# Roots and reciprocals for the norms of a two-block model, gates at eviction and an earlier weight load

## What is computed

```python
def rmsnorm(x, g):
    y = xf * lax.rsqrt(jnp.mean(xf * xf, axis=-1, keepdims=True) + EPS)
# first stack, per layer
    h = rmsnorm(x, g_pre_mix); y = token_mixer(h, ...)      # mLSTM heads and attention, ends in w_out
    x = x + rmsnorm(y, g_post_mix)
    h = rmsnorm(x, g_pre_ffn); y = conv_ffn(h, ...)
    x = x + rmsnorm(y, g_post_ffn)
# second stack, per layer
    ax = modulate(rmsnorm_2(h, norm1_g), mx[0], mx[1])      # then w_in, pooling, attention, retention
    yn = (y - mu) * lax.rsqrt(var + EPS) * gn_g             # retention_output, per head of 64
    ret = silu(gate) * yn                                   # then w_out
    h = h + mx[5] * conv_ffn_2(modulate(rmsnorm_2(h, norm2_g), mx[3], mx[4]), ...)
return rmsnorm_2(h, final_g)
```

## Time and profile before

| | |
|---|---|
| median of three runs | 2932.6 (2928.62 to 2936.35) |
| the profiled execution's own time | 2934.65 |
| its span, first to last instruction | 2932.9 |
| mean granted clock of PE | 0.995 |
| DMA | 269.95 MB, mean 92 GB/s |
| table loads of ACT at L382 | 13, of 1283 ns each |

### The profile page before, as it was taken

One profiled execution on the slowest core, in us unless ns is written; L12 is line 12 of the kernel. 1 busy time (PEld: TensorE's weight loads), 2 busy tenths in 40 slices (PEclk: granted clock), 3 DMA queues, 4 the chain that ended last, 5 costly groups with the idle time before them and its releaser, 6 DMA issues. The chain is left out here.

```text
span 2932.9 us, 35827 instructions
## 1 busy us (share of the span) xinstructions
PE 2856.3 (97%) x14618; PEld 2408.2 (82%) x14618; DVE 1763.2 (60%) x2639; ACT 1160.9 (40%) x1709; POOL 150.0 (5%) x172
## 2 busy tenths in 40 slices
PE   9999999999999999999988999999999999999999
PEld 7657888878467888889965999999999975788887
DVE  6667866768567767667665565435534137564563
ACT  5255524443345424342255343213323236543342
POOL 0101000010110000000020100000000002100001
PEclk9999999999999999999999999999999999999999
DMA  5303243343112243326620111121122220232322
GB/s 204 108 15 108 93 134 105 93 130 122 44 59 86 90 147 100 116 85 232 212 66 30 58 58 65 57 73 65 58 58 65 65 97 23 101 101 84 111 83 83
DMA packets 84180, 269.95 MB, mean 92 GB/s; under 512 B 9264, under 2 KB 12208, under 8 KB 83632
## 3 DMA queue, kind: packets, MB, share of 16 engines
q1 hardware_dynamic: 84016, 267.66, 27.9%
HBM read 265.52 MB, written 2.10 MB: 91 GB/s over the span
## 5 line engine op out<-in xcount | busy, mean ns | idle before, releaser
L1011 PE MATMUL PS<-HH,WH 128*128 128x512 f32 (+1 forms) x3032 | 997.9, 366 | 23.7 <-DVE WL L856 8.1
L1011 PE MATMUL PS<-HH,WL 128*128 128x512 f32 (+1 forms) x3032 | 992.9, 364 | 0.0
L1011 PE MATMUL PS<-HL,WH 128*128 128x512 f32 (+1 forms) x3032 | 992.5, 364 | 0.0
L856 DVE TENSOR_TENSOR WL<-STAGE,WH 128x1024 fp32r<-128x1024 f32 (+2 forms) x420 | 482.7, 1151 | 497.5 <-ACT WH L850 497.2
L850 ACT ACTIVATE WH<-STAGE 128x1024 fp32r<-128x1024 f32 (+2 forms) x420 | 407.3, 973 | 621.5 <-DMA STAGE<-in_w_down 274.0
L1011 PEld LDWEIGHTS PS<-HH,WH 128*128 128x128 f32 x3032 | 559.5, 188 | 95.1 <-issue 11.9
L1011 PEld LDWEIGHTS PS<-HL,WH 128*128 128x128 f32 x3032 | 559.9, 188 | 65.4 <-issue 1.9
L1011 PEld LDWEIGHTS PS<-HH,WL 128*128 128x128 f32 x3032 | 559.7, 188 | 64.7
L1011 PE MATMUL PS<-GH,WL 128*128 128x512 f32 (+1 forms) x880 | 294.7, 367 | 0.0
L1011 PE MATMUL PS<-GL,WH 128*128 128x512 f32 (+1 forms) x880 | 294.7, 367 | 0.0
L1011 PE MATMUL PS<-GH,WH 128*128 128x512 f32 (+1 forms) x880 | 294.6, 367 | 0.0
(11 more groups left out here) (233 smaller groups left out, 2544.9 us busy)
## 6 DMA issues: line engine op xcount, KB each, us to landing
STAGE<-in_w_up SPq DMA_DIRECT2D x176, 512.0 KB, 3.3
MODBUF<-in_w_mod SPq DMA_DIRECT2D x96, 512.0 KB, 4.2
STAGE<-in_w_in SPq DMA_DIRECT2D x84, 512.0 KB, 3.4
STAGE<-in_w_down SPq DMA_DIRECT2D x64, 384.0 KB, 3.1
STAGE<-in_w_down SPq DMA_DIRECT2D x64, 320.0 KB, 2.9
STAGE<-in_w_out SPq DMA_DIRECT2D x32, 512.0 KB, 4.7
BM<-in_na_bias SPq DMA_DIRECT2D x24, 256.0 KB, 2.6
CR<-in_const_ret SPq DMA_DIRECT2D x2, 1152.0 KB, 5.2
```

The lines of the kernel that those rows point to most:

```text
L856: dve.tensor_tensor(WL[unit.slot][:, 0:size], STAGE[unit.slot][:, 0:size], WH[unit.slot][:, 0:size].bitcast(F32), ALU.subtract).then_inc(w ...
L1011: ins = pe.matmul(self.acc(tile, col, tn), w[:, c:c + P], r[:, k, t0:t0 + tn], start=(k == 0 and m == 0), stop=(k == seg.kc - 1 and m == 2))
```

## The change

- In `Rstd`, ACT takes a square root and DVE a reciprocal of RSTD in place; the same in `MixHead` and `RetentionHead`. The table set asked for is `sqrt_and_others` instead of `natural_log`, at fewer places. What waited for the logarithm waits for the root.
- `in2` evicts the three gate tiles through Silu (`store_gates`) instead of Copy, and the Silu of `RetentionHead` goes. The exp set is asked for at the end of `in2`.
- `attention_and_retention` gets the next `Run` and loads its first four units in its tail; unit 0 is also split there. PTN0 and PWM move to slot 2's start.
- Orders: the pooling products go before the last but one retention product; the mean of a late norm goes before chunk 2 of its tile instead of chunk 4; the third tile runs three chunks behind for 768 tokens too; the modulation products of in2(0) are 2 for the first two tiles and 4 for the others.

```diff
 class Rstd:
-                act.activation(RSTD[:, 0:n], PS[2][:, 0:n], ACT.Ln, bias=EPSC[:, 0:1]).then_inc(log_done.sem, 1)
-                act.wait_ge(log_done.sem, log_done.at(self.n + 1))
-                act.activation(RSTD[:, 0:n], RSTD[:, 0:n], ACT.Exp, scale=-0.5).then_inc(rstd_done.sem, 1)
+                act.activation(RSTD[:, 0:n], PS[2][:, 0:n], ACT.Sqrt, bias=EPSC[:, 0:1]).then_inc(root_done.sem, 1)
             def wait(self, eng):
+                eng.wait_ge(root_done.sem, root_done.at(self.n + 1))
+                eng.reciprocal(RSTD[:, 0:self.tokens], RSTD[:, 0:self.tokens]).then_inc(rstd_done.sem, 1)
                 eng.wait_ge(rstd_done.sem, rstd_done.at(self.n + 1))
 class MixHead, act and dve:
-                act.activation(MEAN2, MEAN2, ACT.Ln, scale=float(D // P)).then_inc(head_ln.sem, 1)
+                act.activation(MEAN2, MEAN2, ACT.Sqrt, scale=float(D // P)).then_inc(head_root.sem, 1)
                 self.copied(act, 3)
-                act.wait_ge(head_ln.sem, head_ln.at(1))
-                act.activation(MEAN2, MEAN2, ACT.Exp, scale=-0.5).then_inc(head_rstd.sem, 1)
...
+                dve.wait_ge(head_root.sem, head_root.at(1))
+                dve.reciprocal(MEAN2, MEAN2).then_inc(head_rstd.sem, 1)
                 self.low(dve, 3)
 class RetentionHead, act:
-                act.activation(Z[:, RG:RG + 3, 0:n], Z[:, RG:RG + 3, 0:n], ACT.Silu).then_inc(gate_done.sem, 1)
-                act.preload_act_table_set("natural_log")
                 self.copied(act, 0)
                 self.copied(act, 1)
-                self.run.split_high(act, 0)
...
-                    act.activation(GROUP[c][:, 0:n], PS[VAR_PS[c]][:, 0:n], ACT.Ln,
-                                   bias=EPSC[:, 0:1]).then_inc(group_ln.sem, 1)
+                    act.activation(GROUP[c][:, 0:n], PS[VAR_PS[c]][:, 0:n], ACT.Sqrt,
+                                   bias=EPSC[:, 0:1]).then_inc(group_root.sem, 1)
                 self.run.split_high(act, 2)
-                for c in range(3):
-                    act.wait_ge(group_ln.sem, group_ln.at(c + 1))
-                    act.activation(GROUP[c][:, 0:n], GROUP[c][:, 0:n], ACT.Exp, scale=-0.5).then_inc(group_rstd.sem, 1)
 class RetentionHead, dve:
-                self.low(dve, 0)
-                self.run.split_low(dve, 0)
-                for c in range(1, 5):
+                for c in range(5):
                     self.low(dve, c)
                 self.run.split_low(dve, 1)
-                self.run.split_low(dve, 2)
-                dve.wait_ge(gate_done.sem, gate_done.at(1))
                 for c in range(3):
+                    dve.wait_ge(group_root.sem, group_root.at(c + 1))
+                    dve.reciprocal(GROUP[c][:, 0:n], GROUP[c][:, 0:n]).then_inc(group_rstd.sem, 1)
...
+                    if c == 0:
+                        self.run.split_low(dve, 2)
 Run.tensor:
-                        behind = 3 if self.opening else 0
+                        behind = 0 if i or head.begins else 3 if self.opening or seg.tokens == TOK else 0
...
-                                if t == 0 and k == 4 and i == 0 and head.late:
+                                if t == 0 and k == 2 and i == 0 and head.late:
 PoolPrep.act:
+                if tile.ends:
+                    act.preload_act_table_set("exp_and_others")
 attention_and_retention, sync, then scalar and vector:
                     sp.wait_ge(rest_in.sem, rest_in.at(32))
+                    ahead.loaded = 4
+                    sp.wait_ge(pv_done.sem, pv_done.at(U))
+                    ahead.load(sp, 0)
+                    ahead.load(sp, 1)
+                    sp.wait_ge(masked.sem, masked.at(4 * PAIRS))
+                    ahead.load(sp, 3)
+                    sp.wait_ge(y_ps.sem, y_ps.at(1))
+                    ahead.load(sp, 2)
...
+                        if s == U - 1:
+                            act.preload_act_table_set("sqrt_and_others")
                         if s == U + 1:
                             pooled()
+                            ahead.split_high(act, 0)
...
+                    ahead.split_low(dve, 0)
 store_gates, new, in in2's second segment:
+            def put(act, t, acc):
+                if t < RG - N2_KV:
+                    return other(act, t, acc)
+                return act.activation(by_bank(Z[:, t + N2_KV, 0:tokens], tokens), acc, ACT.Silu)
 in2:
-                            mods=None if l else lambda t: 4 if t < 8 else 3),
+                            mods=None if l else lambda t: 2 if t < 2 else 4),
```

More of the change, by code:

```diff
@@ L246, in build @@
         ysq_done, ysq_added = S("ysq_done"), S("ysq_added")
-        log_done, rstd_done = S("log_done"), S("rstd_done")
+        root_done, rstd_done = S("root_done"), S("rstd_done")
         xsq_done, xsq_summed = S("xsq_done"), S("xsq_summed")
@@ L379, in act, with wait_root @@
                 n = self.tokens
-                act.activation(RSTD[:, 0:n], PS[2][:, 0:n], ACT.Ln, bias=EPSC[:, 0:1]).then_inc(log_done.sem, 1)
-                act.wait_ge(log_done.sem, log_done.at(self.n + 1))
-                act.activation(RSTD[:, 0:n], RSTD[:, 0:n], ACT.Exp, scale=-0.5).then_inc(rstd_done.sem, 1)
-            def wait_log(self, eng):
-                eng.wait_ge(log_done.sem, log_done.at(self.n + 1))
+                act.activation(RSTD[:, 0:n], PS[2][:, 0:n], ACT.Sqrt, bias=EPSC[:, 0:1]).then_inc(root_done.sem, 1)
+            def wait_root(self, eng):
+                eng.wait_ge(root_done.sem, root_done.at(self.n + 1))
             def wait(self, eng):
+                eng.wait_ge(root_done.sem, root_done.at(self.n + 1))
+                eng.reciprocal(RSTD[:, 0:self.tokens], RSTD[:, 0:self.tokens]).then_inc(rstd_done.sem, 1)
                 eng.wait_ge(rstd_done.sem, rstd_done.at(self.n + 1))
@@ L581, in begin @@
                             ins.then_inc(var_ps.sem, 1)
-                        pe.wait_ge(group_ln.sem, group_ln.at(3))
+                        pe.wait_ge(group_root.sem, group_root.at(3))
                     for k in range(5):
@@ L592, in build @@
         ROWS2 = [PO, PO + 1, NV, NV + 1, NV + 2, RG, RG + 1, RG + 2]
-        mean_ps, centred, group_sq, var_ps, group_ln, group_rstd, group_out, gate_done = (
-            S(n) for n in ("mean_ps", "centred", "group_sq", "var_ps", "group_ln", "group_rstd", "group_out", "gate_done"))
+        mean_ps, centred, group_sq, var_ps, group_root, group_rstd, group_out = (
+            S(n) for n in ("mean_ps", "centred", "group_sq", "var_ps", "group_root", "group_rstd", "group_out"))
         def scale_y(dve, gain, c):
@@ L744, in pe @@
                 if self.gain:
-                    self.first.wait_log(pe)
+                    self.first.wait_root(pe)
                     for c in range(DC):
@@ L1149, in stream @@
             if parts[0][0].ready:
-                done(head_ln=1, head_rstd=1, head_ps=4, hg_done=4, head_out=4)
+                done(head_root=1, head_rstd=1, head_ps=4, hg_done=4, head_out=4)
             elif parts[0][0].begins:
-                done(mean_ps=3, centred=3, group_sq=3, var_ps=3, group_ln=3, group_rstd=3, group_out=6, gate_done=1)
+                done(mean_ps=3, centred=3, group_sq=3, var_ps=3, group_root=3, group_rstd=3, group_out=6)
             done(**{f"w_loaded{s}": 16 * len(range(s, n, ring)) for s in range(ring)}, w_hi=n, w_lo=n, unit_done=n,
@@ L1156, in stream @@
                  sq_done=run.n_sq, sq_added=run.n_added, sq_summed=run.n_summed,
-                 ysq_done=run.n_ysq, ysq_added=run.n_ysum, log_done=run.n_rstd,
+                 ysq_done=run.n_ysq, ysq_added=run.n_ysum, root_done=run.n_rstd,
                  rstd_done=run.n_rstd, xsq_done=run.n_x, xsq_summed=run.n_x, t_done=run.n_t, h_hi=run.n_h,
@@ L1192, in build @@
         qk_own, conv_done, qk_done = S("qk_own"), S("conv_done"), S("qk_done")
-        head_ln, head_rstd, head_ps, hg_done, head_out = (
-            S(n) for n in ("head_ln", "head_rstd", "head_ps", "hg_done", "head_out"))
+        head_root, head_rstd, head_ps, hg_done, head_out = (
+            S(n) for n in ("head_root", "head_rstd", "head_ps", "hg_done", "head_out"))
         ROWS1 = [AQ1, AQ1 + 1, AQ1 + 2, AQ1 + 3, V1, V1 + 1, V1 + 2, V1 + 3]
@@ L1212, in pe @@
                 if tile.t == 7:
-                    tile.seg.head.late.wait_log(pe)
+                    tile.seg.head.late.wait_root(pe)
                     pe.wait_ge(acc_free.sem, acc_free.at(tile.n - 6))
@@ L1665, in build @@
         VTN = st("VTN", [P, 9, 3 * P])
-        PTN0 = st("PTN0", [P, 2, SEQ])
-        PWM = st("PWM", [P, 2, P])
+        PTN0 = sb("PTN0", [P, 2, SEQ], offset=o_slot[2])
+        PWM = sb("PWM", [P, 2, P], offset=o_slot[2] + 2 * SEQ * 4)
         BM = [sb(f"BM{i}", [P, 2 * PAIR], offset=o_slot[3] + i * 2 * PAIR * 4) for i in range(4)]
@@ L1773, in build, with attention_and_retention @@
         KE = CS[:, C_KE:C_KE + 4]
-        def attention_and_retention(tokens, VEC, layer):
```

(27 more changed lines are left out.)

4 lines of the change are left out of this document (1 added, 3 removed).

## The result

The changed kernel takes **2985.7 us** (median of 4 runs, 2982.8 to 2986.8) against 2933.4 of the kernel before beside it: ratio 1.0179, 95% interval 1.0163 to 1.0195. That is 52.3 us slower, where +42 was forecast. The profiled execution took 2986.0 with a span of 2984.3, so 51.4 of span over the one before; its mean granted clock is 0.985, before 0.995.

What follows compares the result with a forecast made beforehand. TensorE, busy 97%, was taken as the bound, with what is left at the seams. 20.1 + 7.2 + 9.5 + 4.6 + 2.4 - 1.6 = +42 on 2934.7 gave 2977, against the median 2975 us; range 2914 to 2999.

Steps and rivals of the forecast that it cites:

- Rate of the reciprocal: VectorE's reciprocal in place of Exp: 6.3 ns an element, 3.38 us for 128x512 and 4.99 us for 128x768.
- Nine seams: Nine places where a root mean square stands between TensorE and its next matmul: together +20.1 us.
- rival 1: Reciprocal runs at the rate of other VectorE operations, 0.69 and 0.96 us: -16, 2917 us; chance 0.19.
- rival 2: Reciprocal makes eight passes for an element, 4.4 and 6.5 us: +62, 2995 us; chance 0.18.
- rival 3: Cheap middle, reciprocal at 4.2 ns an element, 2.3 and 3.4 us: 2951 us; chance 0.57 together with the forecast.
- rival 4: The change doesn't do what it says: tables still reload between Sqrt and Square or Identity; chance 0.02.
- Clock: Half clock after longer pauses at the six seams a stream follows, part of it in the pause: 1.2 each, +7.2 us.
- RetentionHead, layer 0: Three reciprocals in turn on VectorE before low(5), on which chunk 5 waits: +8.3 us and 1.2 of clock.
- PE then starts at about 1597.6: RetentionHead, layer 0: TensorE starts at 1597.6 instead of 1598.58, its variance products at 1602.75 instead of 1604.40.
- Layer 1: RetentionHead in layer 1, the same three reciprocals in turn: +3.4 us and 1.2 of clock.
- Gates at eviction: End of in2: load back to exp after the last eviction, ahead of the block's barrier: 1.2 twice, +2.4 us.
- Orders: Pauses of 1.33 and 1.60 us go; against it at most 1.5 at three heads: -1.6 us with 0.2 of rounding.

Runs made afterwards that it cites:

- run 4: Whole model left out, only VectorE reciprocals and adds of 2 to 768 elements: reciprocal 6.25 ns an element from 128 up.
- Run 1: The kernel before with the square roots and reciprocals alone: 2993.98 us, ratio 1.0204.
- run 5: The changed kernel with more idle TensorE matmuls ahead of the seams (42, 37 or 30 calls for 24): 2968.68 us, ratio 1.0122 to the kernel before.
- run 9: The kernel of run 8 with the load back to the exp set moved to the attention block's front: 2911.31 us, ratio 0.9926 to the kernel before.
- run 10: The kernel before with one table set for Ln and Exp and the change's three orders: 2916.22 us, ratio 0.9936.
- run 8: The changed kernel with all inverse roots as Ln and Exp from one table set: 2917.67 us, ratio 0.9949 to the kernel before.
- run 3: The kernel before with one table set for Ln and Exp, two second preloads left out: 2918.38 us, ratio 0.9942.
- run 11: The kernel of run 9 once more, on the same chip as run 10: 2913.34 us, ratio 0.9932 to the kernel before.

## Why the prediction came out as it did

- **Rate of the reciprocal: right, by luck as much as by rows.** 3.38 and 4.99 us were taken, 3.35 and 4.95 measured. But the reasoning (two elements of the one cost as much as eight of the other) rests on 2-element rows that run 4 shows to lie off the line. The middle of two bounds happened to hold; only a wide row could have shown it.
- **Nine seams: right.** +20.1 against +19.7; root to first use +1.62 for a forecast +1.70. Run 1 has the same waits (14.4 and 10.4) without the rest of the change.
- **Rivals:** the row of 3.35 us for 512 elements refutes rivals 1 (0.69), 2 (4.4) and 3 (2.3); rival 4 is refuted by the loads that are gone. The time alone could not have done it: 2985.7 lies 10.7 from the forecast of 2975 and 9.3 from rival 2's 2995. The row tells them apart.
- **Clock: mechanism right, size wrong.** The step that failed: "Part of the slow stretch then lies in the pause itself: 1.2 each". The alignment has 13.2 behind the six seams, 2.2 each, and run 5 takes 11.8 of it away without moving the seams. These 6.0 are most of the 9 us by which the sum was short. The stretches there are 3.4 or 6.8 us long, where the one row of before that I took was 3.4.
- **RetentionHead, layer 0: +12.2 for +9.5.** From the first root to chunk 5 the forecast was 22.9 us and the trace has 22.9 (1628.11 to 1650.99). The step that failed is "PE then starts at about 1597.6": less what had been lost by then (20.4), TensorE's first product is at 1600.0, 1.4 later than before and not 1.0 earlier. The pause at the block's end grew to 3.62 (2.58 before), and the 12 mean products behind it ran partly at half clock: 6.74 us in place of 4.11. Layer 1: +5.0 for +4.6.
- **Gates at eviction: right** (+1.29 twice for +1.2), and run 9 shows that the price was avoidable.
- **Orders:** -1.6 was forecast, the streams gained 3.7; the waits named are gone. The cost of 1.5 set against them does not show. By medians the gain can't be told from clock (run 10).
- **What I did not see:** that the wait of 1.34 in the earlier trace rows could be taken without leaving ScalarE. My sum only asked what the new operations cost.

## What to carry to other kernels

When a table load stands between two functions, first look for one set that holds both; only then move a function to another engine, and price the replacement at its full width, since rows of a few elements say nothing of the rate. A new instruction in front of a seam costs twice: in the wait, and in the clock of the matmuls behind it, which idle matmuls through the whole wait won back here (11.8 of 13.2). Where one engine makes several chunks in turn, put each chunk's last step directly behind it.

## What the runs showed of the hardware that I had not expected

- Idle matmuls through the whole wait are worth 13.4 us of 52 (run 5, aligned), with seams that start no earlier: TensorE's clock stays at 2.4 GHz where it otherwise is at 1.2 for 3.4 to 6.8 us at and behind a wait of 3 to 5.
- Half-clock stretches in the mixers and attention blocks differ between profiles of kernels whose edits don't touch them (in the second mixer, 10.2 us long in the kernel before and in runs 8 and 10, 3.4 in runs 3, 9 and 11). What sets their length is open, and so is whether it changes from one execution of a kernel to the next: run 9's four executions took 2908.0 to 2914.5 us, at mean clocks of 0.999 to 0.996. Two profiles side by side can't show what an edit of some 2 us is worth, unless they are aligned and the stretches are set apart.
- A reciprocal of 2 elements takes 160 ns and of 32 only 300; from 128 (894 ns) to 768 each further element costs 6.25 ns (run 4).
